# Mixture-of-experts stage of a hybrid RWKV-7 / sparse-attention layer: blocks of 32 rows in four column groups of TensorE, with a block's down product issued behind the next block's gate and up product

## The reference, cut to what matters

```
group = argmax of 4 group logits; 2 best of its 8 experts; 2048 assignments (token, expert, weight)
for each of the 32 experts, over its assigned tokens xb:
    hid = silu(xb @ e_gate[e]) * (xb @ e_up[e])        # 1024 -> 512, twice
    y   = hid @ e_down[e]                              # 512 -> 1024
out[token] += weight * y                               # two rows for each token
```

## Time and profile before

| | |
|---|---|
| time, median of 3 runs | 1875.81 us |
| the 3 runs | 1875.81, 1869.55, 1876.41 us |
| span of the profiled execution | 1869.1 us |
| TensorE matmul busy | 1629.8 us (87% of the span) |
| VectorE / ScalarE / GpSimd busy | 50% / 30% / 20% |
| clock granted to TensorE, mean | 0.949 of full speed |
| first gate product of the experts' stage | 1208.8 us |
| end of the last down product | 1811.4 us |
| HBM read / written | 303.2 MB / 38.8 MB |

### The profile page before, as it was taken

The page is one execution under the profiler, slowest core; times in us unless marked ns, Lnnn a source line. Parts: engine busy times, 40 slices in busy tenths (PEclk is TensorE's granted clock), DMA queues, the critical chain, the costliest instruction groups (busy, mean ns, idle before and its releaser), DMA issues. The chain is left out here.

```text
span 1869.1 us, 40718 instructions
## 1 busy us (share of the span) xinstructions
PE 1629.8 (87%) x16070; PEld 1075.9 (58%) x16071; DVE 937.1 (50%) x2046; ACT 559.8 (30%) x1099; POOL 369.4 (20%) x825
## 2 busy tenths in 40 slices
PE   4999999876788889888886898498999999999976
PEld 2744444336666667676664455365666666666652
DVE  4257686346768777768562224432233333333326
ACT  4115887723334434434332112010111111111121
POOL 7301457701101100101000000111111111111110
PEclk8999999988899999999997999599999999999997
DMA  9513434320013011000002563599999799978735
GB/s 332 164 60 150 162 127 167 121 86 27 13 28 106 14 38 28 13 28 18 19 8 75 192 218 137 224 352 408 405 398 366 285 385 388 366 294 313 285 138 230
DMA packets 131649, 334.88 MB, mean 179 GB/s; under 512 B 14174, under 2 KB 52110, under 8 KB 130497
## 3 DMA queue, kind: packets, MB, share of 16 engines
q1 hardware_dynamic: 122496, 314.12, 44.6%
q0 software_dynamic: 9024, 19.00, 3.5%
HBM read 303.23 MB, written 38.82 MB: 183 GB/s over the span
## 5 line engine op out<-in xcount | busy, mean ns | idle before, releaser
L2043 PE MATMUL psX<-arena 128*64 128x256 f32 x1536 | 180.0, 388 | 14.2 <-DMA arena<-in_e_down_dram 12.6
L2067 PE MATMUL psP<-arena 128*64 128x512 f32 x768 | 175.4, 599 | 0.0
L2043 PEld LDWEIGHTS psX<-arena 128*64 128x64 f32 x1536 | 115.2, 140 | 91.4 <-issue 43.5
L806 PE MATMUL psP<-arena 128*128 128x512 f32 x320 | 141.1, 595 | 4.4 <-DVE arena L712 2.9
L506 ACT ACTIVATE arena<-arena 128x1024 bf16<-128x1024 f32 (+5 forms) x138 | 134.2, 973 | 32.5 <-POOL arena L464 28.6
L806 PE MATMUL psX<-arena 128*128 128x512 f32 x320 | 140.9, 595 | 3.4 <-DVE arena L712 1.9
L1740 PE MATMUL psP<-arena 128*128 128x512 f32 x256 | 116.4, 613 | 9.8 <-PEq L112 4.6
L1918 ACT ACTIVATE arena<-arena 64x1024 f32<-64x1024 f32 x49 | 51.7, 1055 | 237.9 <-PE psT L2029 210.9
L1927 ACT ACTIVATE arena<-psX 128x256 f32<-128x256 f32 x48 | 18.4, 383 | 317.3 <-PE psX L2043 317.3
L1261 PE MATMUL psP<-ckvT,arena 128*128 128x512 f32 (+3 forms) x192 | 79.4, 524 | 33.2 <-DVE st L1100 22.0
L806 PEld LDWEIGHTS psP<-arena 128*128 128x128 f32 x320 | 59.9, 190 | 81.4 <-issue 75.4
(11 more groups left out here) (413 smaller groups left out, 2870.0 us busy)
## 6 DMA issues: line engine op xcount, KB each, us to landing
arena<-in_e_gate_dram SPq DMA_DIRECT2D x32, 2048.0 KB, 9.5
arena<-in_e_up_dram SPq DMA_DIRECT2D x32, 2048.0 KB, 15.2
arena<-in_e_down_dram SPq DMA_DIRECT2D x32, 2048.0 KB, 9.4
arena<-in_ada_w_dram SPq DMA_DIRECT2D x12, 2048.0 KB, 16.4
proj_T<-arena SPq DMA_DIRECT2D x36, 256.0 KB, 2.0
arena<-in_x_dram SPq DMA_DIRECT2D x16, 512.0 KB, 5.7
arena<-in_w_in_dram SPq DMA_DIRECT2D x4, 2048.0 KB, 8.4
arena<-in_final_ada_w_dram SPq DMA_DIRECT2D x4, 2048.0 KB, 12.3
```

What stands on the lines that cost most here:

```text
L806: mm = pe.matmul(psum[b], w[:, k, first:first + P], hT[:, k, 512 * half:512 * half + 512], start=(k == 0), stop=(k == KD - 1))
L2043: mm = pe.matmul(psum["X0"][BLK * h:BLK * h + BLK, 0:DE // 2], xT[:, k, :], gate_w[u][:, k, DE // 2 * h:DE // 2 * (h + 1)], start=(k == 0) ...
L2067: mm = pe.matmul(psum["P0"][BLK * half:BLK * half + BLK, :], hidT[:, f, h, :], down_w[u][:, KE // 2 * h + f, D // 2 * half:D // 2 * (half ...
```

## The change

Blocks hold 32 rows instead of 64, and every expert has at least two. A row of 1024 numbers is gathered and stored as four quarter rows of 256, one on each group of 32 partitions, so that a block fills 128 partitions with 256 numbers each. Gate and up become one group of matmuls (`gate_up`): in each of 8 steps four matmuls of 256 columns go to the four column groups, gate to partitions 0 to 63 and up to 64 to 127 of one PSUM bank. The rows are turned by two transposes and the hidden block by two, all of them issued after the second of the 8 steps. The down product (`down`) is 16 matmuls of 256 columns in four column groups; TensorE computes that of block b-1 behind the gate and up product of block b. ScalarE copies the turned hidden block, VectorE the rest, with one eviction of 128 x 256 for each block. SP waits for the counts of the new order. Routing makes tables for 132 blocks instead of 68, on 128 partitions.

```diff
-BLK = 64
+BLK = 32
+QUARTERS = P // BLK
+QD = D // QUARTERS
 SLOTS = 3
-MAX_BLOCKS = NE + 2 * SEQ // BLK
+MAX_BLOCKS = 2 * NE + 2 * SEQ // BLK
...
-        xn2_d = dram("xn2_rows", (SEQ, D))
-        y_d = dram("expert_rows", (2 * SEQ, D))
+        xn2_d = dram("xn2_rows", (QUARTERS * SEQ, QD))
+        y_d = dram("expert_rows", (QUARTERS * 2 * SEQ, QD))
+        xn2_rows, y_rows = (d.rearrange("(s q) n -> s (q n)", q=QUARTERS) for d in (xn2_d, y_d))
...
-                step(dve.tensor_tensor(more, over(counts, SEQ // BLK - 1), each(steps[:, :], NE), ALU.is_gt))
+                step(dve.tensor_tensor(more, over(counts, SEQ // BLK - 2), each(steps[:, :], NE), ALU.is_gt))
                 step(dve.tensor_reduce(last, more, AX_X, ALU.add))
-                step(dve.tensor_scalar(last, last, 1.0, None, ALU.add))
...
-                link(dve, dve.tensor_tensor(in_row, over(place_f[0], BLK), each(count_f[:, 0:BLK], 2 * NT), ALU.is_equal), "in_row", 0)
-                step(dve.tensor_tensor(in_block, over(place_f[1], ALL_BLOCKS), each(count_f, 2 * NT), ALU.is_equal))
-                link(dve, dve.tensor_tensor(in_block, in_block, over(pair_f.rearrange("p t j -> p (t j)"), ALL_BLOCKS), ALU.mult), "in_block", 0)
+                step(dve.tensor_tensor(in_row, over(place_f[0], BLK), each(count_f[:, 0:BLK], 2 * NT), ALU.is_equal))
+                step(dve.tensor_tensor(in_row, in_row, over(pair_f.rearrange("p t j -> p (t j)"), BLK), ALU.mult))
+                link(dve, dve.tensor_tensor(in_block, over(place_f[1], ALL_BLOCKS), each(count_f, 2 * NT), ALU.is_equal), "in_block", 0)
...
+                step(dve.tensor_scalar(idx_all[:, :], idx_all[:, :], float(QUARTERS), quarter[:, 0:1], ALU.mult, ALU.add))
+                link(dve, dve.tensor_scalar(place_all[:, :], place_all[:, :], float(QUARTERS), quarter[:, 0:1], ALU.mult, ALU.add), "idx_all", 0)
...
-                    mm = pe.matmul(psum["W1"][0:BLK, 0:ALL_BLOCKS], in_row[:, i, :], in_block[:, i, :], start=(i == 0), stop=(i == 2 * NT - 1))
+                    for g in range(QUARTERS):
+                        mm = pe.matmul(psum["W1"][BLK * g:BLK * g + BLK, 0:ALL_BLOCKS], in_row[:, i, :], in_block[:, i, :], start=(i == 0), stop=(i == 2 * NT - 1))
...
+            tanh_g, mid = hid[0:2 * BLK], hid[2 * BLK:P]
+            gate_ps, up_ps = psum["X0"][0:2 * BLK, 0:DE // 2], psum["X0"][2 * BLK:P, 0:DE // 2]
+            rows_ps = psum["T0"][:, 0:QD].rearrange("p (r g w) -> p r g w", r=2, g=QUARTERS)
...
-                    sp.wait_ge(q("up_done1"), end)
+                    sp.wait_ge(q("gate_up_done"), end)
                     load_gate_up(e + SLOTS, u)
-                    sp.wait_ge(q("y_done"), end + 1)
+                    sp.wait_ge(q("y_done"), end)
...
+                for b in range(2):
+                    gather(b, b, None)
+                for b in range(2, 6):
+                    gather(b, b % 2, b - 1)
+                with pool.Fori(0, steady) as i:
                     for j in range(2):
-                        gather(i * 2 + j + 3, 1 - j, i * 2 + j + 2)
                         store(i * 2 + j, j)
-                gather(pairs * 2 + 1, 1, pairs * 2)
-                store(full * 2, 0)
-                gather(pairs * 2 + 2, 0, pairs * 2 + 1)
-                store(full * 2 + 1, 1)
-                pool.wait_ge(q("gathered0"), (pairs + 2) * 16)
-                pool.wait_ge(q("gathered1"), (pairs + 1) * 16)
+                        gather(i * 2 + j + 6, j, i * 2 + j + 5)
+                for b in range(2):
+                    for j in range(2):
+                        store(steady * 2 + (2 * b + j), j)
...
+                def half_tanh(b):
+                    act.wait_ge(q("gate_up_done"), b + 1)
+                    act.activation(tanh_g, gate_ps, ACT.Tanh, scale=0.5).then_inc(q("tanh_done"), 1)
+
+                def take_hidden(b):
+                    act.wait_ge(q("hid_turned"), b + 1)
+                    act.activation(hidT.rearrange("p f h w -> p (f h w)"), psum["W0"][:, 0:P], ACT.Copy).then_inc(q("hidT_ready"), 1)
+
+                take_rows(0, 0, 1, None)
+                take_rows(1, 1, 1, 1)
                 with act.Fori(0, pairs) as i:
                     for j in range(2):
                         b = i * 2 + j
-                        take_rows(b + 1, 1 - j, i + 1 + j)
-                        act.wait_ge(q("gate_done"), b + 1)
-                        act.wait_ge(q("hid_turned1"), b + 1)
-                        act.activation(hid, psum["X0"][:, 0:DE // 2], ACT.Tanh, scale=0.5).then_inc(q("tanh_done"), 1)
+                        half_tanh(b)
+                        take_rows(b + 2, j, i + 2, b + 2)
+                        take_hidden(b)
 
                 act.wait_ge(q("y_ready"), pairs * 2 + 1)
...
+                    dve.wait_ge(q("turned"), b + 1)
+                    dve.tensor_tensor(xs, rows_ps, of_pairs(1), ALU.mult).then_inc(q("xs_ready"), 1)
+
+                def shift_rows(b, before):
+                    if before is not None:
+                        dve.wait_ge(q("gate_up_done"), before)
+                    dve.wait_ge(q("xs_ready"), b + 1)
+                    dve.tensor_tensor(xT, xs, of_pairs(0), ALU.add).then_inc(q("xT_ready"), 1)
+
+                def gated(b):
+                    dve.wait_ge(q("tanh_done"), b + 1)
+                    dve.scalar_tensor_tensor(out=mid, in0=tanh_g, scalar=1.0, in1=gate_ps, op0=ALU.add, op1=ALU.mult).then_inc(q("half_gated"), 1)
+                    dve.wait_ge(q("half_gated"), b + 1)
+                    dve.scalar_tensor_tensor(out=mid, in0=mid, scalar=0.5, in1=up_ps, op0=ALU.mult, op1=ALU.mult).then_inc(q("hidden"), 1)
 
                 def evict(b, j, stored):
...
+                    dve.wait_ge(q("y_done"), b + 1)
                     if stored is not None:
                         dve.wait_ge(q(f"y_stored{j}"), stored)
...
+                    dve.tensor_tensor(y_sb[j], y_ps, gate_quarter, ALU.mult).then_inc(q("y_ready"), 1)
+
+                def period(b):
                     scale_rows(b + 1)
+                    shift_rows(b + 1, b + 1)
+                    gated(b)
 
                 scale_rows(0)
...
+                shift_rows(0, None)
+                period(0)
+                period(1)
+                dve.wait_ge(q("gate_quarter"), 16 * QUARTERS)
+                for j in range(2):
+                    evict(j, j, None)
+                    period(j + 2)
+                with dve.Fori(0, steady) as i:
+                    for j in range(2):
+                        evict(i * 2 + j + 2, j, (i + 1) * 16)
+                        period(i * 2 + j + 4)
+                for j in range(2):
+                    evict(steady * 2 + j + 2, j, (steady + 1) * 16)
...
+                    for r in range(2):
+                        mm = pe.transpose(psum["T0"][:, P * r:P * r + P], rows.rearrange("q (p r) -> q r p", r=2)[:, r, :], ident[:, :])
                     mm.then_inc(q("turned"), 1)
 
+                def turn_hidden(b):
+                    for f in range(KE // 2):
+                        mm = pe.transpose(psum["W0"][:, 2 * BLK * f:2 * BLK * f + 2 * BLK], mid[:, P * f:P * f + P], ident[2 * BLK:P, 2 * BLK:P])
+                    mm.then_inc(q("hid_turned"), 1)
+
+                def gate_up(b, u, nth, earlier):
+                    pe.wait_ge(q(f"gate_loaded{u}"), nth)
+                    pe.wait_ge(q(f"up_loaded{u}"), nth)
+                    pe.wait_ge(q("xT_ready"), b + 1)
+                    if earlier:
+                        pe.wait_ge(q("hidden"), b)
+                    for j in range(KD):
+                        r, g = j // QUARTERS, j % QUARTERS
+                        if j == 2:
+                            if earlier:
+                                turn_hidden(b)
+                            turn_rows(b + 1)
+                        for c_ in range(QUARTERS):
+                            w, h = (gate_w, up_w)[c_ // 2][u], c_ % 2
+                            mm = pe.matmul(psum["X0"][BLK * c_:BLK * c_ + BLK, 0:DE // 2], xT[:, r, g, :], w[:, 2 * g + r, DE // 2 * h:DE // 2 * (h + 1)],
+                                           start=(j == 0), stop=(j == KD - 1))
+                    mm.then_inc(q("gate_up_done"), 1)
+
+                def down(b, u, nth):
+                    pe.wait_ge(q(f"down_loaded{u}"), nth)
+                    pe.wait_ge(q("hidT_ready"), b)
+                    pe.wait_ge(q("y_ready"), b)
+                    for i in range(KE):
+                        f, h = i // 2, i % 2
+                        for g in range(QUARTERS):
+                            mm = pe.matmul(psum["P0"][BLK * g:BLK * g + BLK, 0:QD], hidT[:, f, h, :], down_w[u][:, KE // 2 * h + f, QD * g:QD * g + QD],
+                                           start=(i == 0), stop=(i == KE - 1))
+                    mm.then_inc(q("y_done"), 1)
+
+                def expert(e, u, nth, before):
+                    first, end = bounds(pe, e)
```

(80 more changed lines are left out.)

102 lines of the change are left out of this document (33 added, 69 removed).

## The result

The changed kernel takes 1821.09 us (median of 4 runs, 1819.66 to 1826.69) against 1875.07 for the kernel before: a ratio of 0.9728, 95% interval 0.9712 to 0.9744, 54 us less. The forecast was 1827. Five more runs beside a later experiment gave 1823.55, ratio 0.9720 (0.9699 to 0.9740). The profiled execution has a span of 1817.9 us, against 1869.1 before.

What follows compares the result with a forecast made beforehand. Two limits were named: TensorE at 12.15 us a block and weights costing 19.5 us. 1377 + 61 x 6.3 + 1 = 1762 for the blocks' end gave span 1820, median 1827 us; range 1803 to 1868, the forecast's own 1803 to 1848.

Steps and rivals of the forecast that it cites:

- Start of the stage: Routing before the experts' blocks: larger tables and matmul add about 5 us, so the first gate product starts near 1213.8.
- Period: TensorE, one 32-row block: gate and up 3.42, down 1.71, turns 1.0, loop 0.17, sum 6.3 us against 12.15 for 64 rows.
- Loop and bounds on TensorE's sequencer: TensorE's loop turn and bound reads may show behind the shorter down product: 0 to 2.6 us a block, 0.17 taken.
- The cover of the chain: Between blocks: the 1.71 us down product hides the 1.45 us chain from tanh to hidden values, 0.26 to spare.
- Rival 2: Hidden-value chain doesn't fit behind down: with 0.5 us a block open, period 6.8 and 1854 us; chance 0.08.
- Weights: Expert weight loads: 16.6 us an expert, 15 us wait up to expert 11 plus 2 for the clock, then weights ahead.
- End: End of the experts' blocks: 1762 us against 1811.4 before, 49 us less.
- Packets (rival 1): DMA queues: a 1 KB packet costs as much as a 2 KB one, an expert takes 18.5 us, 1868 us; chance 0.12.
- Stores (rival 3): Store landings through two buffers set the period from 9.5 us on; at 11 us period 7.05, time 1875; chance 0.05.
- Loop (rival 4): TensorE's loop turn and bound reads open behind down: period 7.1 us; at 1.5 us open 7.6 and 1921 us; chance 0.10.
- three groups (rival 5): Gate, up and down: four column groups overlap only as three, period 8.0 us, time 1955 us; chance 0.03.

Runs made afterwards that it cites:

- the added step: One more VectorE step of 64 x 256, result unused, between tanh and the first hidden-value step of the kernel after: 1839.39 us, 0.9823 of the kernel before.
- the last version: Kernel after with TensorE's experts written out, one bound read each, and one block for experts of at most 32 rows: 1798.69 us, 0.9605 of the kernel before.
- the version with one block alone: Kernel after with one block instead of two for an expert of at most 32 rows, nothing else changed: 1809.71 us, 0.9674 of the kernel before.

## Why the prediction was right

The prediction's direction and mechanism hold. Its span of 1820 us for 1817.9 is closer than its terms, some of which were off in opposite directions.

- **Start of the stage.** Predicted 1213.8 us, 5 later than before; the first gate product is at 1210.4. Routing, from the comparison of the counts to the last index table, takes 17.8 us instead of 14.7, 3.1 more and not 5: the matmul (L1792) with its hand-over takes 1.45 more, not 3.6. That the tables end 5.3 us later all the same is luck, for routing itself began 2.1 later in this execution (1183.3 for 1181.1; it is up to 1188.4 in the experiments). Why isn't shown. From there to the gate product it is 9.3 us instead of 13.0, which the prediction left out: copy, transposes and the two scaling steps work on 256 numbers a partition instead of up to 1024, and the gather lands 1.2 us sooner.
- **Period.** Predicted 6.3 us: 3.42 and 1.71 of matmuls, 1.0 of turns, 0.17 of loop. Measured 6.05 inside an expert, with 3.42, 1.73 and 0.85 to 0.9, and nothing for the loop; and 0.7 to 1.3 us more at each expert, 18.5 us or 0.30 a block over the 61 late ones. The sum, 6.35, agrees, but in part by luck: the turns were put 0.1 too high, and the 0.17 was a choice between 0 and 2.6 that no row of before narrowed. The step "Loop and bounds on TensorE's sequencer" named the right place and held two things of different price: the turn of the loop over blocks costs nothing, the bounds and the loop over three all of it.
- **The cover of the chain.** Predicted 0.26 us to spare, measured 0.06 with the added step. The prediction counts the down product and the chain from the same moment, but down's first record starts while the last ones of gate and up still run: in the block above down starts at 1509.71 and tanh at 1509.96, 0.25 later (line below). Rival 2, at 0.08, was nearer than its chance says.
- **Weights.** Predicted 16.6 us an expert, expert 11's gate and up landing at 1375 and a wait of 15 us with 2 for the clock; measured 16.6, 1371.2, and 10.6 us of waits in all, 12 with the clock by the run without the down matrices. Predicted wait and clock, 17, were 5 too much. The first refill went out at 1222.7, not 1226, which explains the landing. Behind expert 11 no wait: as predicted.
- **End.** Predicted 1762 for the end of the blocks; the last down product ends at 1762.9. Against before that is 48.5 less (49 predicted), and 49.6 at the reload.
- **Packets (rival 1).** The value taken (no dearer than before) was right, its reason was not. The queue's 9024 packets were not two for each 4 KB row. From 1250 to 1760 us nearly all of its bytes go in packets of 4096, 3598 of them before and 3749 after, and most other packets have 4 bytes or, after, 16; 2.1 KB was the mean of the two sorts. If the quarter rows went as packets of their own, there would be 16384 of 1 KB more. The page's count of packets under 2 KB rises by 414 (52110 to 52524) and the queue's by 240, to 9264, at 3.1% of 16 x 1817.9 us or 97 ns each. So the quarter rows travel together here.
- **Stores (rival 3).** A store lands 5.7 us after its issue, 7.1 at most, and a gather after 5.7 and 6.8, well inside two periods; VectorE never waited for one. GpSimd's instruction went from 0.93 to 0.97 us to 1.02 to 1.05 for twice the indices.
- **Loop (rival 4) and three groups (rival 5).** The first is excluded by the period of 6.05, the second by 54 ns a record and by the run with two groups.

The start of tanh in the block above, and the landings of stores and gathers in the kernel after, from issue (L1904 and L1894):

```profile
1509.96 0.38 ACT L1936 ACTIVATE arena<-psX 64x256 f32<-64x256 f32 x1 [2.92 <-PE psX L2065]
```

```profile
DMA to landing us min/median/max: 2.1/5.7/7.1
```

```profile
DMA to landing us min/median/max: 2.8/5.7/6.8
```

## What to carry to other kernels

Before changing the size of a block, work out the price of a row of room at each size: here it is 0.19 us at both, so what a smaller block gains is the room that stays empty, and only a shape that keeps the price (four column groups; with two, a block takes 8.6 us for 6.05) lets it. Price the new shape from any line of the old trace that has it: the adaLN matmuls on 128*32 tiles gave this change's main term to 2%. When a product is made half as long, look at what the sequencer did unseen behind it: two reads of bounds directly in front of a gate product cost some 11 us here (20 times 0.55), and one read behind the product costs nothing that shows. And where work is put behind other work to cover a chain, measure the margin with an added step: a cover of 0.06 us works, but nothing more fits under it.

## What the runs showed of the hardware

- Idle time of 1.54 and 0.41 us in each block of 8.2 was enough to make TensorE's granted clock fall to its lower level in part of the blocks (0.88 over 100 us). In the kernel with two added steps TensorE stands idle for 0.66 us in each block of 6.9, and the clock stayed as high as in the kernel after (0.949 and 0.948 over the execution).
- Records on different column groups overlap across products as well: with gate and up in two passes, the down product's first records ran on groups 0 and 1 while the last records of gate and up ran on 2 and 3.
- A loop's turn on TensorE over a body of 48 matmuls (96 records) and 4 transposes left no gap, while two reads of a register from SBUF directly in front of a matmul left 0.55 us (6.6 less 6.05).
- A branch past a loop, where it was taken, was followed in the last version by a gap of 2.1 to 3.5 us inside the next gate product, three times of three, and in the version with one block alone by 5.7, 1.4 and next to nothing. The cause isn't shown.
- Gathers and stores of quarter rows of 1 KB went in packets of 4096 bytes, as rows of 4 KB did (3749 and 3598 of them in the same stretch), and the queue's count rose from 9024 to 9264 only.
